# Expert layer of a streaming encoder: v rows of tiles 1 to 5 by a product with the whole v table

## The chip, the core and the metric

The kernel runs on one core of a Trainium2 chip. The metric is the device time of one execution in microseconds.

## The reference

One layer, run for 1024 prompt tokens and 32 sample tokens with the same weights: a retention and a short convolution in parallel heads, an output projection onto the residual, and then the expert layer, which is most of the work:

```python
q = (xb @ wq).reshape(PEER_BLOCK, PEER_HEADS, 2, D_KEY_HALF)
...
top_s, sel = lax.top_k(cand, PEER_TOPK)
eidx = jnp.take_along_axis(cidx, sel, axis=-1)
gate = jax.nn.softmax(top_s.astype(jnp.float32), axis=-1).astype(xb.dtype)
act = jax.nn.gelu(jnp.einsum('td,thkd->thk', xb, u_tab[eidx]))
return jnp.einsum('thk,thkd->td', gate * act, v_tab[eidx])
```

Each token has 8 heads with 16 experts each, 128 in all, out of 16384; an expert is a row of u and a row of v, each 1024 fp32. An index is `i1 * 128 + i2`. A last RMS norm follows.

## The kernel before, in words

Tokens lie on the 128 partitions: tiles 0 to 7 of the prompt, and the sample tile of 32. The expert work is a run of 1056 steps, 128 for each prompt tile and 32 for the sample tile, whose tokens are spread over the partitions four times. In step `g` GpSimd gathers, by an indirect DMA, the u and v rows of one expert for each token of the tile (128 rows of 8 KB, u and v side by side in `uv`) into a row buffer (L985). VectorE multiplies the u half by the normed token and sums it (L2050, one custom instruction and a read of its accumulator). ScalarE takes the gelu of the dot (L1225), multiplies it by the gate (L1241) and scales the v half by it (L1245). TensorE adds that half, transposed in eight pieces, into the PSUM tile `expert_sum` (L1625). When TensorE is through, the buffer is free and GpSimd may gather into it again. There are seven row buffers in `ring`, and from step 616 nine, two of them in `w_out_sb`.

All else is laid between these steps. Each engine has generators that `yield` the step (the code calls it slot) at which they are to go on, and `advance(programs, g)` runs what is due at step `g`; on each engine the order is fixed by these numbers. The projections of the mixing part (L1311, L1344), the output projection (L1406), the queries (L1508) and key scores (L1537) of the later tiles, VectorE's choice of the 16 best (L1852 to L1982) and the weights that SyncE loads for them through three `stream` buffers are such work. Tiles 0 and 1, then 2 to 4, then 5 to 7 with the sample, form groups that are projected together. At the end of a tile `finish(t)` turns the sum back, norms it and SyncE stores it.

```python
for g in range(TOTAL):
    t, k = tile_of(g)
...
    dve.wait_ge(landed[SLOTS[g]], 16 * (lap_of(g) + 1))
    u = row_of(g)[:, 0:D]
    dve.tensor_tensor_reduce(u, u, xn[:, t % 2, :], 1.0, 0.0, ALU.mult, ALU.add,
                             dots[:, SLOTS[g]:SLOTS[g] + 1]).then_inc(dotted, 1)
    advance(programs, g)
```

## Time and profile before

| | us |
|---|---|
| median of 3 executions | 2945.24 (2944.16 to 2946.45) |
| span of the profiled execution | 2941.5 |
| VectorE busy | 2077.7 (71%) |
| TensorE's matmuls busy | 2311.9 (79%) |
| ScalarE busy | 1968.4 (67%) |
| GpSimd busy | 1258.5 (43%) |

The profiled execution is known by its span, from its first to its last instruction; its own time as a run is not listed beside it, so the median is set against the span: 3.7 us lie between them. An engine's busy time is the union of its instructions. Idle time of an engine is put down to what ended it.

### The profile page before, as it was taken

What the parts mean: (1) busy time and instruction counts of PE and PEld (TensorE: products, weight loads), DVE (VectorE), ACT (ScalarE), POOL (GpSimd) and SP (SyncE); (2) the same over time, 40 slices, a digit from 0 to 9 for tenths busy, and PEclk for the clock granted to TensorE, in tenths of its full rate; (3) what the DMA queues carried; (4) which work ended last, traced back from release to release, by engine and by line L of the source; (5) the groups of instructions that cost most, each with busy time, mean ns of one, the idle gap of its engine ahead of it and who ended that gap; (6) DMA issues with size and microseconds to landing.
All of it is one profiled execution on the core that took longest, in us unless ns stands there. A gap on an engine that the chain in (4) does not pass through costs nothing.

```text
span 2941.5 us, 36244 instructions
## 1 busy us (share of the span) xinstructions
PE 2311.9 (79%) x12548; PEld 1815.8 (62%) x12548; DVE 2077.7 (71%) x5143; ACT 1968.4 (67%) x3670; POOL 1258.5 (43%) x1063
## 2 busy tenths in 40 slices
PE   9988988987787777888987888778766666666777
PEld 8877777665565556665665555555655555555556
DVE  3677788675687887777666555788868787766444
ACT  2477666677676777666667676777767666767663
POOL 0233434444343444344444445334444445555653
PEclk9999999999987879999996988988767656666669
DMA  8899999999999999999999999999999999999998
GB/s 340 323 408 404 419 416 407 414 418 421 420 409 415 416 416 411 421 420 409 419 415 410 419 421 420 420 420 420 418 421 421 418 418 413 412 419 410 421 413 338
DMA packets 182055, 1205.73 MB, mean 410 GB/s; under 512 B 21744, under 2 KB 27184, under 8 KB 43504
## 3 DMA queue, kind: packets, MB, share of 16 engines
q0 software_dynamic: 152368, 1107.36, 91.2%
q1 hardware_dynamic: 29264, 95.93, 8.4%
q8 instruction: 99, 1.62, 0.2%
q14 instruction: 84, 0.69, 0.1%
q10 hardware_dynamic: 240, 0.13, 0.0%
HBM read 1198.48 MB, written 4.86 MB: 409 GB/s over the span
## 4 chain that ended last, share of the span: by engine, by line
DMA 42%; PE 22%; DVE 21%; ACT 10%; issue 4%; POOL 1%; SPq 0%; DVEq 0%; ACTq 0%; POOLq 0%
DMA ring<-in_uv,idx 38%; PE expert_sum L1625 9%; DVE ring L2050 9%; ACT ring L1245 4%; DMA w_out_sb<-in_uv,idx 4%; PE x_ps L1406 2%; PE mm L1508 2%; PE mm L1311 1%; ACT weights L1241 1%; PE x_ps L1344 1%; PE mm L1344 1%; DVE pairs_left L1855 1%; ACT L1225 1%; PE x_ps L1311 1%; PE expert_sum L1311 1%
## 5 line engine op out<-in xcount | busy, mean ns | idle before, releaser
L985 POOL DMA_INDIRECT ring<-in_uv,idx x958 | 1137.1, 1187 | 1534.0 <-PE expert_sum L1625 1328.1
L1625 PE MATMUL expert_sum<-ident_sb,ring 128*128 128x128 f32 x7472 | 1222.4, 319 | 516.6 <-ACT ring L1245 513.7
L2050 DVE CUSTOM_DVE_ANT_0 ring<-ring,xn 128x1024 f32<-128x1024 f32 x959 | 1168.1, 1222 | 616.9 <-DMA ring<-in_uv,idx 610.8
L1625 PEld LDWEIGHTS expert_sum<-ident_sb,ring 128*128 128x128 f32 x7472 | 1022.3, 165 | 782.5 <-ACT ring L1245 711.7
L1245 ACT ACTIVATE ring<-ring,weights 128x1024 f32<-128x1024 f32 x934 | 1073.0, 1149 | 30.4
L1225 ACT ACTIVATE dots<-dots 128x1 f32<-128x1 f32 x1056 | 211.4, 200 | 789.8 <-DVE dots L2050 786.9
L1241 ACT ACTIVATE weights<-dots,gate 128x1 f32<-128x1 f32 x1024 | 301.5, 294 | 38.3 <-DVE gate L1994 1.5
L1508 PE MATMUL mm<-xn_in,stream 128*128 128x416 f32 (+1 forms) x500 | 202.9, 531 | 0.0
L1625 PE MATMUL expert_sum<-ident_sb,w_out_sb 128*128 128x128 f32 x720 | 139.2, 358 | 70.0 <-ACT w_out_sb L1245 69.8
L1625 PEld LDWEIGHTS expert_sum<-ident_sb,w_out_sb 128*128 128x128 f32 x720 | 113.6, 186 | 98.7 <-ACT w_out_sb L1245 96.3
L985 POOL DMA_INDIRECT w_out_sb<-in_uv,idx x96 | 115.8, 1206 | 124.9 <-PE expert_sum L1625 110.4
L2050 DVE CUSTOM_DVE_ANT_0 w_out_sb<-w_out_sb,xn 128x1024 f32<-128x1024 f32 x97 | 118.5, 1223 | 68.3 <-DMA w_out_sb<-in_uv,idx 67.7
L1311 PE MATMUL mm<-stream,xn_in 128*128 128x256 f32 (+1 forms) x640 | 166.4, 395 | 0.0
L1311 PEld LDWEIGHTS mm<-stream,xn_in 128*128 128x128 f32 (+1 forms) x640 | 106.8, 182 | 22.4 <-issue 4.2
L1508 PEld LDWEIGHTS mm<-xn_in,stream 128*128 128x128 f32 x500 | 91.4, 204 | 40.9 <-issue 27.1
L1245 ACT ACTIVATE w_out_sb<-w_out_sb,weights 128x1024 f32<-128x1024 f32 x90 | 103.4, 1149 | 2.9
L2050 DVE DVE_READ_ACCUMULATOR2_ANT dots<- 128x1 f32 x1056 | 86.8, 82 | 0.0
L1344 PE MATMUL mm<-xn_in,stream 128*128 128x384 f32 (+1 forms) x232 | 84.3, 496 | 2.6 <-ACT conv_tmp L1028 2.3
L1225 ACT ACT_TABLE_LOAD x50 | 64.2, 1283 | 0.9
L1311 PE MATMUL x_ps<-stream,xn_in 128*128 128x256 f32 x256 | 64.0, 383 | 0.0
L1344 PE MATMUL x_ps<-xn_in,stream 128*128 128x128 f32 (+1 forms) x240 | 60.8, 400 | 0.0
L1571 PE MATMUL mm<-ring,stream 128*128 128x256 f32 x200 | 50.0, 399 | 9.3 <-ACT stream L1231 9.3
(405 smaller groups left out, 2218.3 us busy)
## 6 DMA issues: line engine op xcount, KB each, us to landing
stream<-in_wq SPq DMA_DIRECT2D x21, 1024.0 KB, 11.7
stream<-in_w_conv SPq DMA_DIRECT2D x16, 1024.0 KB, 11.3
stream<-in_w_ret SPq DMA_DIRECT2D x16, 1024.0 KB, 9.5
ring<-in_uv,idx POOLq DMA_INDIRECT x958, 13.9
ring<-in_w_ret SPq DMA_DIRECT2D x6, 1024.0 KB, 12.5
x<-in_x SPq DMA_DIRECT2D x8, 512.0 KB, 8.3
out_y<-xn SPq DMA_DIRECT2D x8, 512.0 KB, 8.2
stream<-in_w_out SPq DMA_DIRECT2D x3, 1024.0 KB, 9.7
```

Source lines behind the costliest of these rows:

```text
L985: pool.indirect_dma_start(row_of(g), None, uv, bass.IndirectOffsetOnAxis(ap=rows, axis=0)).then_inc(landed[SLOTS[g]], 16)
L1225: act.activation(d, d, ACT.Gelu_apprx_tanh).then_inc(gelu_done, 1)
L1241: act.activation(w, d, ACT.Copy, scale=gate[:, t % 5, k:k + 1]).then_inc(weighed, 1)
L1245: act.activation(v, v, ACT.Copy, scale=w).then_inc(scaled, 1)
L1311: ins = pe.matmul(bank[0:n, 0:UNIT], xnj[:, k, at:at + n], weight[k], start=(k == 0), stop=(k == KC - 1))
L1344: ins = pe.matmul(bank[:, 0:columns.stop - columns.start], weight[k], moving, start=(k == 0), stop=(k == KC - 1))
L1406: ins = pe.matmul(x1_ps[0:n, i * 512:(i + 1) * 512], lhsT, w_out_of(j, k)[:, i * 512:(i + 1) * 512], start=(k == 0), stop=(k == KC - 1))
L1508: ins = pe.matmul(query_bank(m, s), weight[s][k], xnT_of_pass(m)[:, k, :], start=(k == 0), stop=(k == KC - 1))
L1571: ins = pe.matmul(last_bank, of[0:rows, 96 - q * DEC:96 - q * DEC + P], values[0:rows, q * QW:(q + 1) * QW], start=begins and q == 0, stop ...
L1625: ins = pe.matmul(expert_sum[:, c * P:(c + 1) * P], row_of(g)[:, D + c * P:D + (c + 1) * P], ident_sb[:, :], is_transpose=True, start=Fals ...
L1855: ins = dve.match_replace(rest, values[:, 0:8], s, LOWEST)
L2050: dve.tensor_tensor_reduce(u, u, xn[:, t % 2, :], 1.0, 0.0, ALU.mult, ALU.add, dots[:, SLOTS[g]:SLOTS[g] + 1]).then_inc(dotted, 1)
```

## The change

For tiles 1 to 5 (`DENSE`, steps 128 to 767) only the u half is gathered: `uv` is seen as 32768 rows of 4 KB, the chosen indices of these tiles are doubled, and eight half buffers in the first four row buffers hold them. VectorE writes the dots of a tile into the columns of `tile_dots`; ScalarE and TensorE do nothing in these steps. In the next tile's time (in tile 6 for tile 5) the spread weights of a tile are built. The indices are split into their two halves, these and the weights (gelu of the dot by the gate) are transposed, and for each token ScalarE makes a one-hot of the first half (`hot_1`, as relu(1 - |iota - i1|)), GpSimd one of the second that carries the weight (`hot_2`), and TensorE multiplies them: the result is that token's 16384 weights, with the second half of the index on the partitions. It goes by groups of four tokens. ScalarE copies it into `staging`, SyncE stores 32 tokens at a time (2 MB, in pieces of 512 B) into a table in DRAM. x1 of tiles 1 to 4 is kept in DRAM too.

From step 826 on TensorE multiplies the spread weights of the five tiles by the whole v table, in 32 chunks of 512 rows: 320 units (chunk, tile, half of the columns) of four matmuls of 128x512, of which `unit_at` puts three into every two steps. VectorE adds each unit from PSUM to the tile's sum, which starts as x1. SyncE loads a chunk of v (2 MB) and the spread weights of each chunk and tile (256 KB). At the end ScalarE and VectorE norm the five sums and SyncE stores them. The three row buffers that the building takes leave six for the full rows of steps 768 to 825, and seven after that. Tiles 0, 6, 7 and the sample are handled as before.

How GpSimd's instructions stand: its queue before, from its first gather on (`in_uv` is the table, `idx` the indices, 128x2048 a full row of each partition).

```order
L985 DMA ring<-in_uv,idx 128x2048 x623
L985 DMA w_out_sb<-in_uv,idx 128x2048 x2
L985 DMA ring<-in_uv,idx 128x2048 x7
L985 DMA w_out_sb<-in_uv,idx 128x2048 x2
L985 DMA ring<-in_uv,idx 128x2048 x7
```

GpSimd's queue in the change, from its first gather into tile 2. The `ring<-ring` rows are the weighted one-hots, which lie in the last three row buffers.

```order
L1180 DMA ring<-in_uv,idx 128x2048 x128
L1159 DMA ring<-in_uv,idx 128x1024 x137
L1130 ISA
L1130 TENSOR_SCALAR ring<-ring 128x128 x4
L1159 DMA ring<-in_uv,idx 128x1024 x3
L1130 TENSOR_SCALAR ring<-ring 128x128 x4
L1159 DMA ring<-in_uv,idx 128x1024 x4
L1130 TENSOR_SCALAR ring<-ring 128x128 x4
L1159 DMA ring<-in_uv,idx 128x1024 x4
```

Full gathers end with tile 0, and from tile 2 on four one-hots stand in the same queue after every three or four gathers, so that a gather waits for them and they for it.

TensorE before, around steps 824 to 832: only the transposes of the rows.

```order
L1625 MATMUL expert_sum<-ident_sb,w_out_sb 128x128 x16
L1625 MATMUL expert_sum<-ident_sb,ring 128x128 x56
L1625 MATMUL expert_sum<-ident_sb,w_out_sb 128x128 x16
```

TensorE in the change, steps 822 to 830 (`tp` is the PSUM pair of the product, `stream` and `ring` hold v, `xn_in` and `qkvg` the spread weights).

```order
L1925 MATMUL expert_sum<-ident_sb,ring 128x128 x32
L1871 MATMUL tp<-stream,xn_in 128x512 x8
L1925 MATMUL expert_sum<-ident_sb,ring 128x128 x8
L1871 MATMUL tp<-stream,xn_in 128x512 x4
L1925 MATMUL expert_sum<-ident_sb,ring 128x128 x8
L1871 MATMUL tp<-stream,xn_in 128x512 x8
L1925 MATMUL expert_sum<-ident_sb,ring 128x128 x8
```

Two units or one now stand ahead of each step's eight transposes.

The diff, cut to its core:

```diff
+DENSE = (1, 2, 3, 4, 5)
+FULL = [t for t in range(TILES + 1) if t not in DENSE]
...
+GROUP4 = 4
+GROUPS4 = P // GROUP4
...
+CHUNK = 4
+CHUNKS = NK // CHUNK
+UNITS = CHUNKS * len(DENSE) * 2
+V_DEEP = 2
+W_DEEP = 6
...
+def build_at(t):
+
+    return (t + 1) * STEPS + 1
+
+
+def group4_at(t, q):
+
+    return build_at(t) + 3 + ((q * 15) // 4 if t != DENSE[-1] else (q * 3) // 2)
+
+
+BUILT = group4_at(DENSE[-1], GROUPS4) + 4
+DENSE_AT = BUILT + 2
+
+
+def unit_at(n):
+
+    return DENSE_AT + (n * 2) // 3
...
+RINGS = [(0, tuple(range(RING))), (DENSE_END, (0, 1, 2, 3, RING, RING + 1)),
+         (BUILT + 2, (0, 1, 2, 3, RING, RING + 1, 4))]
...
+        work = ring[:, 4:7, :].rearrange("p s n -> p (s n)")
+        staging = work[:, 0:NK * BLOCK]
+        hot_1 = work[:, 4096:4608].rearrange("p (t n) -> p t n", t=GROUP4)
+        hot_2 = work[:, 4608:5120].rearrange("p (t n) -> p t n", t=GROUP4)
+        halves_i = work[:, 4608:4864].bitcast(I32).rearrange("p (s n) -> p s n", s=2)
+        halves_f = work[:, 4864:5120].rearrange("p (s n) -> p s n", s=2)
+        tile_dots = work[:, 5120:5376].rearrange("p (b n) -> p b n", b=2)
+        turned_w = work[:, 5376:5760].rearrange("p (s n) -> p s n", s=3)
+        iota_sb2 = work[:, 5760:5888]
+        v_rows = [stream[:, 1:3, :].rearrange("p b (i n) -> p (b i) n", i=2),
+                  ring[:, 5:7, :].rearrange("p b (i n) -> p (b i) n", i=2)]
+        w_rows = [xn_in[:, D + i * CHUNK * P:D + (i + 1) * CHUNK * P] for i in range(4)]
+        w_rows += [qkvg[:, 2, i * CHUNK * P:(i + 1) * CHUNK * P] for i in range(2)]
+        sums = [keys_sb[:, 0:KC, :].rearrange("p b n -> p (b n)"), keys_sb[:, KC:, :].rearrange("p b n -> p (b n)"),
...
+            def store_spread(t):
+
+                for b in range(BLOCKS):
+                    yield group4_at(t, (b + 1) * PER_BLOCK) + 2
+                    i = DENSE.index(t)
+                    sp.wait_ge(w_copied, i * GROUPS4 + (b + 1) * PER_BLOCK)
+                    sp.dma_start(w_spread[i, :, :, b * CHUNK * BLOCK:(b + 1) * CHUNK * BLOCK].rearrange("c p n -> p c n"),
+                                 staging.rearrange("p (c n) -> p c n", c=CHUNKS)).then_inc(w_stored, 16)
...
+            def load_v():
+
+                rows = uv.rearrange("(c i p) n -> c p i n", i=CHUNK, p=P)
+                for c in range(CHUNKS):
+                    yield QUADS_AT_V if c == 0 else BUILT if c == 1 else unit_at((c - 1) * 2 * len(DENSE) - 1) + 1
+                    if c == 0:
+                        sp.wait_ge(queried, 2 * len(PASSES))
+                    elif c == 1:
+                        sp.wait_ge(w_stored, 16 * BLOCKS * len(DENSE))
+                        sp.wait_ge(w_built, GROUPS4 * len(DENSE))
+                    else:
+                        sp.wait_ge(unit_done, (c - 1) * 2 * len(DENSE))
+                    sp.dma_start(v_rows[c % V_DEEP], rows[c][:, :, D:]).then_inc(v_in[c % V_DEEP], 16)
+
+            def load_spread():
+
+                for m in range(CHUNKS * len(DENSE)):
+                    c, i = divmod(m, len(DENSE))
+                    yield BUILT + 1 if m < W_DEEP else unit_at(2 * (m - W_DEEP) + 1) + 1
+                    if m == 0:
+                        sp.wait_ge(w_stored, 16 * BLOCKS * len(DENSE))
+                        sp.wait_ge(queried, 2 * len(PASSES))
+                        sp.wait_ge(chosen, pick(PH - 1, 6) + 1)
+                    elif m >= W_DEEP:
+                        sp.wait_ge(unit_done, 2 * (m - W_DEEP) + 2)
+                    sp.dma_start(w_rows[m % W_DEEP], w_spread[i, c]).then_inc(w_in_rows[m % W_DEEP], 16)
...
+                for q in range(GROUPS4):
+                    yield group4_at(t, q) + 5
+                    if q == 0:
+                        pool.wait_ge(w_turned_copied, 2 * i + 2)
+                        pool.wait_ge(wide_iota, NK // TOPK + 1)
+                    wait(pool, w_built, r + q)
+                    for k in range(GROUP4):
+                        at = GROUP4 * q + k
+                        pool.tensor_scalar(hot_2[:, k, :], iota_sb2[:, :], turned_w[:, 1, at:at + 1],
+                                           turned_w[:, 2, at:at + 1], ALU.is_equal, ALU.mult).then_inc(hot_2_ready, 1)
...
+                if half is not None:
+                    pool.wait_ge(dotted, half + 1)
+                if SLOTS[g] == 4 and g > DENSE_END:
+                    pool.wait_ge(w_stored, 16 * BLOCKS * len(DENSE))
...
+                    pool.indirect_dma_start(half_row_of(g), None, uv.rearrange("n (h d) -> (n h) d", h=2),
+                                            bass.IndirectOffsetOnAxis(ap=idx[:, t % 5, k:k + 1], axis=0)
+                                            ).then_inc(landed[LANDINGS[g]], 16)
...
+                act.activation(tile_dots[:, t % 2, :], tile_dots[:, t % 2, :], ACT.Gelu_apprx_tanh).then_inc(tile_gelu, 1)
...
+                for q in range(GROUPS4 + 1):
+                    yield group4_at(t, q)
+                    if q < GROUPS4:
+                        wait(act, w_built, r + q)
+                        if q == 0:
+                            act.wait_ge(w_turned_copied, 2 * i + 2)
+                        for k in range(GROUP4):
+                            at = GROUP4 * q + k
+                            act.activation(hot_1[:, k, :], iota_sb2[:, :], ACT.Abs,
+                                           bias=turned_w[:, 0, at:at + 1]).then_inc(hot_1_steps, 1)
+                        act.wait_ge(hot_1_steps, (GROUP4 + 1) * (r + q) + GROUP4)
+                        act.activation(hot_1, hot_1, ACT.Relu, bias=one_sb[:, :],
+                                       scale=-1.0).then_inc(hot_1_steps, 1)
+                    if q:
+                        p = q - 1
+                        act.wait_ge(w_built, r + p + 1)
+                        if p % PER_BLOCK == 0:
+                            wait(act, w_stored, 16 * (i * BLOCKS + p // PER_BLOCK))
+                        first = GROUP4 * (p % PER_BLOCK)
+                        act.activation(staging.rearrange("p (c t i) -> p t c i", c=CHUNKS, t=BLOCK)[:, first:first + GROUP4, :, :],
+                                       build_bank(t, p).rearrange("p (t c i) -> p t c i", t=GROUP4, c=CHUNKS),
+                                       ACT.Copy).then_inc(w_copied, 1)
...
+                    pe.wait_ge(hot_1_steps, (GROUP4 + 1) * (r + q + 1))
+                    pe.wait_ge(hot_2_ready, GROUP4 * (r + q + 1))
+                    wait(pe, w_copied, r + q - 1)
+                    for k in range(GROUP4):
+                        ins = pe.matmul(build_bank(t, q)[:, k * NK:(k + 1) * NK], hot_2[:, k, :],
+                                        hot_1[:, k, :], start=True, stop=True)
+                    ins.then_inc(w_built, 1)
...
+                    if i == 0 and h == 0:
+                        pe.wait_ge(v_in[c % V_DEEP], v_in_from[c % V_DEEP] + 16 * (c // V_DEEP + 1))
+                    if h == 0:
+                        pe.wait_ge(w_in_rows[m % W_DEEP], w_in_rows_from[m % W_DEEP] + 16 * (m // W_DEEP + 1))
+                    wait(pe, unit_added, n - 1)
+                    spread_w = w_rows[m % W_DEEP].rearrange("p (t i) -> p t i", i=CHUNK)
+                    for k in range(CHUNK):
+                        ins = pe.matmul(tp[:, n % 2, :], spread_w[:, :, k],
+                                        v_rows[c % V_DEEP][:, k, h * 512:(h + 1) * 512],
+                                        start=(k == 0), stop=(k == CHUNK - 1))
+                    ins.then_inc(unit_done, 1)
...
+                    dve.wait_ge(unit_done, n + 1)
+                    if n == 0:
+                        dve.wait_ge(sums_in, 16 * (len(DENSE) - 1))
+                    if c:
+                        dve.wait_ge(unit_added, n - 2 * len(DENSE) + 1)
+                    half = sums[i][:, h * 512:(h + 1) * 512]
+                    dve.tensor_tensor(half, half, tp[:, n % 2, :], ALU.add).then_inc(unit_added, 1)
...
+                    u = half_row_of(g)
+                    dve.tensor_tensor_reduce(u, u, xn[:, t % 2, :], 1.0, 0.0, ALU.mult, ALU.add,
+                                             tile_dots[:, t % 2, k:k + 1]).then_inc(dotted, 1)
```

## Rows read from the trace of the kernel before

**Rows 1.** The page: DMA share in 40 slices; queues: packets, MB, share.
```profile
DMA  8899999999999999999999999999999999999998
...
q0 software_dynamic: 152368, 1107.36, 91.2%
q1 hardware_dynamic: 29264, 95.93, 8.4%
```

**Rows 2.** The waits: engine, line, what ended it; us, times, longest.
```profile
POOL ring L985 <- PE expert_sum L1625: 1328.1, 807, 5.3
...
DVE ring L2050 <- DMA ring<-in_uv,idx: 610.8, 489, 3.7
...
DVE w_out_sb L2050 <- DMA w_out_sb<-in_uv,idx: 67.7, 55, 2.2
```

**Rows 3.** Windows: bounds, length, busy (count) of PE, PEld, DVE, ACT, POOL; clock; DMA.
```profile
0.00:95.70 95.70, 92.88 (x540) 79.91 (x541) 37.65 (x118) 20.82 (x43) 3.29 (x7) 1.00 0.82 307
...
483.20:830.80 347.60, 286.37 (x1578) 207.62 (x1576) 243.12 (x511) 242.93 (x446) 146.78 (x128) 0.95 1.01 417
830.80:1177.50 346.70, 262.03 (x1426) 205.47 (x1426) 279.12 (x772) 246.41 (x458) 151.03 (x129) 0.83 1.01 413
1177.50:1532.10 354.60, 309.23 (x1755) 230.19 (x1754) 254.90 (x597) 239.09 (x445) 144.41 (x129) 0.97 1.01 417
1532.10:1870.30 338.20, 264.55 (x1367) 188.58 (x1366) 200.42 (x374) 237.32 (x434) 151.78 (x129) 0.85 1.01 418
1870.30:2205.90 335.60, 250.75 (x1324) 191.64 (x1324) 268.21 (x746) 240.67 (x448) 151.20 (x130) 0.82 1.01 420
2205.90:2353.70 147.80, 96.45 (x480) 80.50 (x480) 119.99 (x328) 104.72 (x187) 61.90 (x58) 0.67 1.01 419
2353.70:2894.60 540.90, 375.66 (x1739) 305.76 (x1740) 353.47 (x829) 354.85 (x663) 291.69 (x214) 0.65 1.01 414
```

**Rows 4.** Groups, each shape apart: gathers and dots (busy us, mean ns | idle before).
```profile
L985 POOL DMA_INDIRECT ring<-in_uv,idx x958 | 1137.1, 1187 | 1534.0 <-PE expert_sum L1625 1328.1 <-PE expert_sum L1311 91.0 <-issue 57.8
...
L2050 DVE CUSTOM_DVE_ANT_0 ring<-ring,xn 128x1024 f32<-128x1024 f32 x959 | 1168.1, 1222 | 616.9 <-DMA ring<-in_uv,idx 610.8
L2050 DVE DVE_READ_ACCUMULATOR2_ANT dots<- 128x1 f32 x1056 | 86.8, 82 | 0.0
```

**Rows 5.** Timeline of 3.7 us on GpSimd and VectorE: start, length, instruction.
```profile
1000.72 0.94 POOL L985 DMA_INDIRECT ring<-in_uv,idx  x1 [1.46 <-PE expert_sum L1625]
1002.88 1.48 POOL L985 DMA_INDIRECT ring<-in_uv,idx  x1 [1.23 <-PE expert_sum L1625]
...
1002.32 1.23 DVE L2050 CUSTOM_DVE_ANT_0 ring<-ring,xn 128x1024 f32<-128x1024 f32 x1
```

**Rows 6.** Groups, each shape apart: the nearest rows for the new instructions.
```profile
L971 POOL DMA_INDIRECT ring<-in_uv,spare x1 | 0.9, 936 | 1.5 <-PE mm L1571 1.5
L2123 POOL MEMSET const-float32-0.0<- 128x1 f32 x1 | 0.1, 99 | 0.2 <-issue 0.2
...
L1724 DVE SCALAR_TENSOR_TENSOR conv_tmp<-conv_tmp,par 128x128 f32<-128x128 f32 x16 | 5.6, 352 | 0.6
...
L1781 DVE TENSOR_TENSOR qkvg<-mm,decay_p_sb 128x512 f32<-128x512 f32 x8 | 5.5, 688 | 2.1 <-PE mm L1367 2.1
...
L1153 ACT ACTIVATE scores<-tp 128x256 f32<-128x256 f32 x36 | 13.3, 368 | 1.9 <-PE tp L1537 1.9
...
L1056 ACT ACTIVATE turn<-tp 128x512 f32<-128x512 f32 x16 | 8.6, 589 | 0.4 <-PE tp L1359 0.4
```

**Rows 7.** DMA issues: KB and median us from issue to landing.
```profile
w_out_sb<-in_w_out SPq DMA_DIRECT2D x1, 2048.0 KB, 23.7
```

**Rows 8.** TensorE: matmuls of 512 columns, weight loads, and a step's eight transposes.
```profile
63.83 3.60 PE L1420 MATMUL x_ps<-w_out_sb,qkvg 128*128 128x512 f32 x8
...
L1420 PEld LDWEIGHTS x_ps<-w_out_sb,qkvg x16: 190/190/192, 63.7 to 72.0; 128*128 128x128 f32 x16
...
1001.57 1.04 PE L1625 MATMUL expert_sum<-ident_sb,ring 128*128 128x128 f32 x8
```

More of the change, by code:

```diff
@@ L60, with is_dense, full_before, landing_of @@
 QUADS_IN = 0
+QUADS_AT_V = 780
 SPLIT = 2
-RINGS = [(0, RING), (88 * RING, RING + 2)]
+DENSE = (1, 2, 3, 4, 5)
+FULL = [t for t in range(TILES + 1) if t not in DENSE]
+HALVES = 8
+DENSE_FIRST = DENSE[0] * STEPS
+DENSE_END = (DENSE[-1] + 1) * STEPS
+ROW_SLOTS = RING + 2
+GROUP4 = 4
+GROUPS4 = P // GROUP4
+BLOCK = 32
+BLOCKS = P // BLOCK
+PER_BLOCK = BLOCK // GROUP4
+CHUNK = 4
[11 more added lines that the diff above has]
+    return DENSE_AT + (n * 2) // 3
+def is_dense(g):
+    return DENSE_FIRST <= g < DENSE_END
+RINGS = [(0, tuple(range(RING))), (DENSE_END, (0, 1, 2, 3, RING, RING + 1)),
+         (BUILT + 2, (0, 1, 2, 3, RING, RING + 1, 4))]
 def slot_of(g):
     first, slots = [r for r in RINGS if r[0] <= g][-1]
-    return (g - first) % slots
+    return (g - first) % HALVES if is_dense(g) else slots[(g - first) % len(slots)]
 SLOTS = [slot_of(g) for g in range(TOTAL)]
-def lap_of(g):
-    return SLOTS[:g].count(SLOTS[g])
-def same_slot_before(g):
-    return max((b for b in range(max(0, g - 2 * RING), g) if SLOTS[b] == SLOTS[g]), default=None)
+def full_before(g):
+    return sum(not is_dense(b) for b in range(min(g, TOTAL)))
+def landing_of(g):
+    return SLOTS[g] // 2 + SLOTS[g] % 2 * (HALVES // 2) if is_dense(g) else SLOTS[g]
+LANDINGS = [landing_of(g) for g in range(TOTAL)]
+def lap_of(g):
+    return LANDINGS[:g].count(LANDINGS[g])
+def halves_of(g):
+    return (SLOTS[g],) if is_dense(g) else (2 * SLOTS[g], 2 * SLOTS[g] + 1)
+def steps_before(g):
+    near = {}
+    for b in range(max(0, g - 3 * STEPS * len(DENSE)), g):
+        for half in halves_of(b):
+            near[half] = b
+    found = {near[half] for half in halves_of(g) if half in near}
+    return (max((b for b in found if not is_dense(b)), default=None),
+            max((b for b in found if is_dense(b)), default=None))
+def full_index(t):
+    return sum(u < t for u in FULL)
 def rows_of(t):
@@ L165, in sums_before_out @@
 def sums_before_out(t):
-    return sum(end_of(u) < out_at(t) for u in range(TILES + 1))
+    return sum(end_of(u) < out_at(t) for u in FULL)
 TURNS = [(x_turn_at(t), t, "x") for t in range(TILES + 1)]
@@ L916, in store_y, with store_sums @@
+            def store_sums():
+                yield unit_at(UNITS) + 4
+                for i, t in enumerate(DENSE):
+                    sp.wait_ge(end_step, len(DENSE) + 3 + i)
+                    sp.dma_start(y[t * P:(t + 1) * P, :], sums[i]).then_inc(end_out, 16)
             def store_y(t):
@@ new lines, in end_sums @@
+            def end_sums():
+                yield unit_at(UNITS) + 2
+                act.wait_ge(unit_added, UNITS)
+                for i in range(len(DENSE)):
+                    act.activation(v_rows[i // CHUNK][:, i % CHUNK, :], sums[i], ACT.Square,
+                                   accum_out=end_stat[:, 0, i:i + 1]).then_inc(end_step, 1)
+                act.wait_ge(end_step, len(DENSE))
+                act.activation(end_stat[:, 0, :], end_stat[:, 0, :], ACT.Sqrt, bias=eps_sb[:, :],
+                               scale=1.0 / D).then_inc(end_step, 1)
@@ new lines, in dense @@
+            def dense():
+                for n in range(UNITS):
+                    m, h = divmod(n, 2)
+                    c, i = divmod(m, len(DENSE))
+                    yield unit_at(n)
+                    if n == 0:
+                        pe.wait_ge(keyed_copied, len(SCORES) - 1)
+                        pe.wait_ge(xnT_copied, 2 * len(TURNS))
+                    if i == 0 and h == 0:
[9 more added lines that the diff above has]
+                    ins.then_inc(unit_done, 1)
@@ L1582, in _ @@
+            programs = started(warm_up(), rstd_row(), *[back(t) for t in FULL], *[build(t) for t in DENSE], dense(),
                                *[projection(j) for j in range(len(GROUPS))],
@@ new lines, in end_sums @@
+            def end_sums():
+                yield unit_at(UNITS) + 3
+                dve.wait_ge(end_step, len(DENSE) + 1)
+                dve.reciprocal(end_stat[:, 1, :], end_stat[:, 0, :]).then_inc(end_step, 1)
+                dve.wait_ge(end_step, len(DENSE) + 2)
+                for i in range(len(DENSE)):
+                    dve.scalar_tensor_tensor(sums[i], sums[i], end_stat[:, 1, i:i + 1], g_fin_sb[:, :],
+                                             ALU.mult, ALU.mult).then_inc(end_step, 1)
```

224 lines of the change are left out of this document (174 added, 50 removed).

## The prediction

> **What bounds the kernel now.** I read the page's slices first: the DMA engines are busy for nine tenths or more of every slice but the first two and the last [rows 1]; no compute engine has such a row. The queue lines say whose traffic it is: the gathers' queue holds 91.2% of the engines' time for 1107 MB, so one of 1056 gathers costs 0.912 x 2941.5 / 1056 = 2.54 us; everything else is 96 MB in 8.4%, which is 388 GB/s [rows 1]. The list of waits closes the circle: GpSimd waits 1328 us for TensorE to free a row buffer, and at the other end of the chain VectorE waits 611 + 68 us for rows to land [rows 2]; ScalarE and TensorE follow VectorE. The first cause is the landing. So time before is bytes; the question is what bounds each stretch when the bytes are fewer. I cut the span at the steps where the change has its seams [rows 3]: tile 1, tiles 2 to 5 (one window each), steps 768 to 825 and steps 826 to 1038. In all of them the DMA share is full before; only the first 96 us and what follows step 1038 differ.
>
> **Bytes after.** 640 gathers of half size save 640 x 1.27 = 813 us of DMA time. The v table (67.1 MB), the spread weights written (41.9 MB) and read (41.9 MB) and the kept x1 (4 MB) are 155 MB, at 388 GB/s 400 us. If all stayed DMA bound the span would fall by 413 us. It can't, since the saving lies in tiles 1 to 5 and nearly all of the addition behind step 768, where nothing is saved. Each part therefore has to be costed with its own limit.
>
> **Tiles 1 to 5, VectorE's side.** It still makes each dot: 1.22 us and 0.08 us for the read-out [rows 4]. Nothing else goes from it but the final scaling of each of the five sums, which moves to the end. Its busy time in the five windows is 243.1, 279.1, 254.9, 200.4 and 268.2, in sum 1245.7 of 1722.7 us [rows 3]; that is the floor. Waits for other engines come on top: in the span VectorE is idle for 863.8 us, 678.5 of them for rows; of the other 185 us, 58 lie before the first dot (95.70 - 37.65), and 127 on 2040 busy us are 6%, which I keep.
>
> **Tiles 2 to 5, GpSimd's side.** Here are the weighted one-hots of tiles 1 to 4, 512 instructions of 128x128 (those of tile 5 stand in tile 6). Where GpSimd stands in the way is seen in the timeline [rows 5]: the gather issued at 1000.72, beside a reduce that reads one operand, takes 0.94 us; the one issued at 1002.88, inside a dot that ends at 1003.55, takes 1.48, which is the 0.67 us left of the dot and 0.81. A gather's issue waits until the dot that is running ends. The smaller gathers cost GpSimd no less: those of 4 KB rows take 0.94 us too [rows 6], so the halved rows save nothing there. A one-hot reads SBUF as well, so I let it wait as the gather does. Its own length isn't in the trace: below it lies a memset of one column on GpSimd, 0.1 us, above it a gather's issue, 0.94 us; the nearest row is VectorE's 128x128 operation, 0.35 us [rows 6], and I take that. Whether it then holds up a dot, no row shows: dots keep 1.22 us beside gathers. Bounds are 0 and 0.35 us for each, and I take the upper, since a reader that must wait for a dot is likely to make a dot wait too. The Trainium skill (SBUF — State Buffer, the sections on ports) says that VectorE with two SBUF inputs and a reading GpSimd instruction exclude each other for the whole instruction, whichever came first; by that rule the upper end holds, by the row alone the sum would be 190 us less.
>
> VectorE then needs (1002.6 + 512 x 0.35) x 1.06 = 1253 us for tiles 2 to 5. GpSimd per step: a gather of 0.94 to 1.30 and 0.35 + 0 to 1.22 for the one-hot: 1.29 at best and 2.87 at worst, where each of its instructions stands behind a full dot, against VectorE's 2.45. In the middle it is hidden. Tile 1 has no one-hots: 243.1 x 1.06 = 258. ScalarE and TensorE lose their per-step work here and don't bind; DMA needs 1.27 us a step and 22 us a tile for weights written (8.4 MB). Together **1511 us for 1722.7: -212**.
>
> **Steps 768 to 825.** Full rows again, and tile 5's one-hots in 48 steps, a group of four each step and a half. ScalarE: 104.7 us for 58 steps before [rows 3], 1.8 a step; a group adds four instructions of 128 columns and two of 512. By its 128x256 at 0.37 and 128x512 at 0.59 [rows 6] these are 4 x 0.26 + 2 x 0.59 = 2.2, or 1.5 a step: 3.3 us. GpSimd: 1.2 and 2.67 x (0.35 + 0.3) = 2.9. DMA: 2.54 and 8.4 MB of stores over 48 steps, 0.45: 3.0. Three loads of equal size, coupled through one set of one-hots and a staging buffer that must be stored before it is filled again, with six row buffers in place of nine: I take 4.0 us a step, 232 us, between 3.3 (191) and 4.7 (273). Behind it TensorE stands at the first unit of the product until the last 2 MB store has landed and the first weights have been read back; a 2 MB load takes 23.7 us from issue to landing [rows 7], and I take 25 us in all, between 10 and 40. **257 for 147.8: +109.**
>
> **Steps 826 to 1038: the product with the whole table.** 320 units of four matmuls of 128x512, three units every two steps. Eight such matmuls take 3.60 us, 0.45 each, and a step's eight transposes 1.04 [rows 8]. TensorE: 6 x 0.45 + 1.04 = 3.7 us a step, at the full clock: before, the granted clock was 0.65 here, with TensorE busy for 70% of the time, but 1.00 in the first 96 us, where it was busy for 97% [rows 3]; I expect the latter. DMA: 2.54 + 1.5 x (67.1 + 41.9) MB / 320 / 388 GB/s = 2.54 + 1.32 = 3.86, the larger. VectorE: 1.66 us a step before (353.5 / 213), and 1.5 additions of 0.69 [rows 6], hence 2.7; ScalarE 1.7. With two engines within 4% of each other and seven buffers, 5% are lost to their coupling: 4.05 x 213 = **863 for 540.9: +322**. The bounds are 3.86 (822) and 4.4 (937). The rest, with five squares and five scalings on engines with slack, and five stores of 0.5 MB: 46.9, **+2**.
>
> **Sum.** -212 + 109 + 322 + 2 = +221 on 2941.5, so a span of 3162.5; the median lies 3.7 us above the profiled span, so **3166 us**, 7.5% slower. In short: the change takes 336 MB out of a stretch that at once finds another limit, and 109 MB of streams and 1280 x 0.45 = 576 us of matmul into one that has none to spare.
>
> **Rivals.**
> - *Faster: nothing excludes anything.* One-hots run beside dots without touching them. Then tiles 1 to 5 take 1245.7 x 1.06 = 1320 (-402), steps 768 to 825 take 3.3 x 58 + 15 (+59), the product is at its DMA floor, 822 (+281), +2: -60, 2885 us. For it: the 959 dots have a mean of 1.22, that of the one beside the gather in [rows 5], and GpSimd's issue is 1.19 in the mean [rows 4], 0.25 over the free one. Against it: [rows 5], and that it needs all three at once. It decides for faster once tiles 1 to 5 need less than 2.1 us a step with 3.9 us in the product; VectorE's floor is 1245.7 / 640 = 1.95 (mine: 2.36 and 4.05).
> - *Slower: GpSimd becomes the bound.* VectorE has rows waiting whenever four one-hots come in a row, so each stands behind a full dot: 2.87 x 512 + 258 = 1727 for tiles 1 to 5 (+4), and the rest as above: +437, 3382 us. It decides once a gather and a one-hot together take over 2.45 us. For it: the issues' mean is 1.19 already, with VectorE at dots for 45% of the time (157 of 350 us a tile: 128 x 1.22); at 2.45 us a step it is at them for half. Against: at that pace VectorE is idle for a seventh of the time.
> - *Slower: TensorE becomes the bound of the product.* Its stationary operand steps by four elements; the loads shown step by one and take 0.19 us [rows 8]. If a column that steps by four costs as much as four that step by one, a load is 0.76, when a step takes 6 x 0.76 + 1.04 = 5.6 us, 1193 us in all (+652), 3496 us. The nearest row is the 0.19 itself, which its matmul's 0.45 us hides more than twice over. The Trainium skill (SBUF — State Buffer, the note on cachelines) has 16-byte lines and a penalty for each access that crosses into a new one; by it every fp32 element here is on its own line. No run shows it, and the chance stands at one in twelve. A clock left at 0.65 would come out alike: 3.7 / 0.65 = 5.7 us a step.
>
> **Chances.** My own course 0.62, VectorE untouched 0.13, GpSimd bound 0.15, TensorE bound 0.08, about even 0.02. A range of 2930 to 3400 us leaves out the last and the better part of the fast case. A measurement of this kernel tells 0.2% from no change: faster 0.13, same 0.02, slower 0.85.
>
> **What would show it.** In tiles 2 to 5 dots of 1.22 us with waits for GpSimd's one-hots between them, a pitch near 2.45 us, DMA share about 0.7; gathers' issues of up to 2 us; one-hots in the order of 0.35 us alone. In steps 826 to 1038 a DMA share near 0.95, TensorE's clock at 1.00, loads of stationary operands under 0.45 us, a pitch near 4.05. A pitch below 2.2 in the first, or far from 4 in the second, proves the sum wrong.

## The result

The changed kernel takes 3875.26 us (median of 4, 3867.77 to 3877.41) against 2945.01 us (4 executions, 2944.16 to 2946.45): 1.315 times as long, 95% interval 1.3132 to 1.3169. The forecast was 3166 us with a range of 2930 to 3400. The sign was right, the size was not: of the 930 us that were lost 221 were foreseen, a quarter.

### The profile page after: what moved, and what is told of

Read it like the earlier page. It is cut to its first block, busy times and chain, and to the rows that moved or that the text cites. A ratio compares the mean times of both kernels' runs of the same rounds, so it can differ in the third digit from the quotient of the medians.

```text
span 3873.0 us, 34448 instructions
## 1 busy us (share of the span) xinstructions
PE 2868.9 (74%) x11203; PEld 2132.2 (55%) x11203; DVE 2306.7 (60%) x5493; ACT 1282.2 (33%) x2681; POOL 2054.4 (53%) x1703
## 4 chain that ended last, share of the span: by engine, by line
PE 45%; POOL 11%; issue 10%; DMA 6%; ACT 4%; DVE 4%; SPq 0%; ACTq 0%; DVEq 0%; POOLq 0%
PE tp L1871 29%; POOL ring L1130 6%; POOL ring L1159 5%; PE expert_sum L1925 5%; DMA w_spread<-ring 4%; PE expert_sum L1851 3%; PE mm L1559 2%; PE mm L1756 2%; DMA ring<-in_uv,idx 2%; PE x_ps L1654 2%; ACT ring L1423 2%; DVE ring L2407 1%; PE mm L1818 1%; ACT ring L1426 1%; PE x_ps L1851 1%
## 5 line engine op out<-in xcount | busy, mean ns | idle before, releaser
L1130 POOL TENSOR_SCALAR ring<-ring 128x128 f32<-128x128 f32 x640 | 794.2, 1248 | 39.6 <-PE x_ps L1851 19.6
L1851 PE MATMUL expert_sum<-ring 128*128 128x128 f32 x1024 | 225.4, 390 | 627.2 <-issue 558.5
L1851 PEld LDWEIGHTS expert_sum<-ring 128*128 128x128 f32 x1024 | 195.6, 285 | 682.3 <-issue 651.7
L1925 PE MATMUL expert_sum<-ident_sb,ring 128*128 128x128 f32 x2480 | 350.5, 289 | 86.0 <-ACT ring L1493 85.1
L1871 PE MATMUL tp<-stream,xn_in 128*128 128x512 f32 x864 | 392.3, 604 | 28.9 <-DMA xn_in<-w_spread 28.9
L1925 PEld LDWEIGHTS expert_sum<-ident_sb,ring 128*128 128x128 f32 x2480 | 308.8, 150 | 165.3 <-ACT ring L1493 100.3
L1871 PE MATMUL tp<-ring,xn_in 128*128 128x512 f32 x864 | 390.1, 601 | 0.0
L1493 ACT ACTIVATE ring<-ring,weights 128x1024 f32<-128x1024 f32 x310 | 356.2, 1149 | 10.1
L1423 ACT ACTIVATE ring<-ring 128x128 f32<-128x128 f32 x640 | 203.4, 390 | 394.3 <-PE expert_sum L1851 341.1
L1871 PEld LDWEIGHTS tp<-stream,xn_in 128*128 128x128 f32 x864 | 261.7, 310 | 120.4 <-issue 32.7
L1871 PEld LDWEIGHTS tp<-ring,xn_in 128*128 128x128 f32 x864 | 261.2, 310 | 87.2
```

Source lines behind the costliest of these rows:

```text
L1130: pool.tensor_scalar(hot_2[:, k, :], iota_sb2[:, :], turned_w[:, 1, at:at + 1], turned_w[:, 2, at:at + 1], ALU.is_equal, ALU.mult).then_in ...
L1423: act.activation(hot_1[:, k, :], iota_sb2[:, :], ACT.Abs, bias=turned_w[:, 0, at:at + 1]).then_inc(hot_1_steps, 1)
L1493: act.activation(v, v, ACT.Copy, scale=w).then_inc(scaled, 1)
L1851: ins = pe.matmul(build_bank(t, q)[:, k * NK:(k + 1) * NK], hot_2[:, k, :], hot_1[:, k, :], start=True, stop=True)
L1871: ins = pe.matmul(tp[:, n % 2, :], spread_w[:, :, k], v_rows[c % V_DEEP][:, k, h * 512:(h + 1) * 512], start=(k == 0), stop=(k == CHUNK - 1))
L1925: ins = pe.matmul(expert_sum[:, c * P:(c + 1) * P], row_of(g)[:, D + c * P:D + (c + 1) * P], ident_sb[:, :], is_transpose=True, start=Fals ...
```

## The profile after

The page of the changed kernel: TensorE's matmuls, GpSimd, the granted clock and the DMA share in 40 slices, and the queues.

```profile
PE   9889878344366674655553255599999999999998
...
POOL 0343256598889988998989777311221112222212
PEclk9999988666678886767766566699999999999999
DMA  8999988767577676767666767767667667667666
...
q0 software_dynamic: 152368, 771.82, 54.8%
q1 hardware_dynamic: 152592, 251.13, 18.0%
```

Where [rows 1] had a full DMA row, no slice behind the fifth is full now. GpSimd holds the stretch from the ninth to the 22nd slice, TensorE everything behind the 26th. Both engines were the bound of a rival of the forecast, though TensorE for another reason than the one given there. The windows, cut at the same steps as [rows 3] (tiles 1, 2, 3, 4, 5, steps 768 to 825, steps 826 to 1038, the rest; columns as there):

```profile
488.40:756.90 268.50, 176.58 (x547) 101.22 (x545) 238.69 (x509) 32.39 (x56) 162.88 (x133) 0.82 0.85 307
756.90:1119.30 362.40, 169.54 (x635) 126.33 (x635) 285.65 (x784) 103.44 (x253) 314.62 (x255) 0.68 0.65 220
1119.30:1478.10 358.80, 246.45 (x960) 169.61 (x961) 258.81 (x601) 103.86 (x245) 320.16 (x256) 0.84 0.71 245
1478.10:1829.20 351.10, 184.76 (x616) 111.99 (x615) 202.62 (x378) 102.11 (x241) 315.17 (x257) 0.70 0.71 237
1829.20:2197.20 368.00, 149.30 (x524) 104.77 (x523) 273.79 (x749) 95.56 (x237) 320.49 (x256) 0.65 0.64 217
2197.20:2464.50 267.30, 142.37 (x717) 128.54 (x718) 122.87 (x329) 174.62 (x375) 185.18 (x185) 0.67 0.73 266
2464.50:3814.80 1350.30, 1321.43 (x4276) 973.74 (x4275) 558.70 (x1147) 356.64 (x662) 274.74 (x215) 0.99 0.68 251
3814.80:3873.00 58.20, 44.16 (x167) 34.84 (x165) 28.40 (x45) 22.48 (x68) 17.38 (x15) 0.91 0.70 270
```

| stretch | before | forecast | after | pitch after |
|---|---|---|---|---|
| tile 0 and what is ahead of it | 483.2 | 483.2 | 488.4 | |
| tile 1 | 347.6 | 258 | 268.5 | 2.10 |
| tiles 2 to 5 | 1375.1 | 1253 | 1440.3 | 2.81 |
| steps 768 to 825 | 147.8 | 257 | 267.3 | 4.61 |
| steps 826 to 1038 | 540.9 | 863 | 1350.3 | 6.34 |
| the rest | 46.9 | 49 | 58.2 | |

Of the 709 us between forecast and result, 487 lie in the product's stretch and 187 in tiles 2 to 5; the four other lines make up 35. "Steps 768 to 825" is not as good a hit as it looks: the forecast of 257 was 232 for the steps (4.0 us each) and 25 for TensorE's wait ahead of the first unit. That wait falls behind step 826, in the product's 1350.3 us, so the 267.3 us are the steps alone.

What GpSimd does, its groups in the changed kernel over the whole span (busy us, mean ns of one, idle before); the 640 gathers of half rows take in tile 1, the 640 one-hots steps 768 to 825:

```profile
L1159 POOL DMA_INDIRECT ring<-in_uv,idx x640 | 762.3, 1191 | 270.4 <-issue 158.3 <-DVE ring L2407 92.6 <-PE expert_sum L1925 18.9
L1130 POOL TENSOR_SCALAR ring<-ring 128x128 f32<-128x128 f32 x640 | 794.2, 1248 | 39.6 <-PE x_ps L1851 19.6 <-PE expert_sum L1851 8.2 <-ACT ring L1410 6.5
```

and the same line by its durations (min/median/max in ns):

```profile
L1130 POOL TENSOR_SCALAR ring<-ring x640: 780/805/4635, 763.9 to 2447.6; 128x128 f32<-128x128 f32 x160
```

A one-hot takes 0.80 us when nothing is in its way, and 1.25 in the mean over all 640. Over tiles 2 to 5 alone the mean is 1.31, with 1.18 for the gather. With 0.33 us of idle time for each step (1440.3 - 1270.4 busy in four tiles, over 512 steps) that is the pitch of 2.8.

What lengthens a one-hot can be counted in the trace. The 237 beside which no dot ran took 0.80 us in the mean. The 226 that began while a dot was running took 1.82, and the middle one of them ended 0.67 us behind the end of that dot. The same holds for the issue of a gather in the kernel before: 449 began while a dot was running, and half of them ended 0.811 to 0.813 us behind its end. So one row of [rows 5] had the rule right for the gather. The timeline shows both kinds, four one-hots in 4.34 us and two in 3.30:

```profile
1303.75 1.09 POOL L1159 DMA_INDIRECT ring<-in_uv,idx  x1 [0.31 <-issue]
1304.88 4.34 POOL L1130 TENSOR_SCALAR ring<-ring 128x128 f32<-128x128 f32 x4
1309.38 1.03 POOL L1159 DMA_INDIRECT ring<-in_uv,idx  x1 [0.17 <-issue]
...
1316.07 3.30 POOL L1130 TENSOR_SCALAR ring<-ring 128x128 f32<-128x128 f32 x2
```

The waits of tile 3, the longest first (1119.3 to 1478.1 us; engine, what it was about to work on <- what came last, us in total, times, longest), say the same from the other side:

```profile
PEld expert_sum L1851 <- issue: 93.7, 24, 8.3
...
DVE ring L2407 <- DMA ring<-in_uv,idx: 64.2, 32, 5.8
```

L1851 is the matmul with a one-hot. The 24 waits ahead of it, up to 8.3 us, are put down to "issue", with no releaser shown; the code has it wait there for `hot_1_steps`, `hot_2_ready` and `w_copied`, and which of them came last is for the experiments. VectorE's wait for rows here is not a wait for bytes: with the DMA share at 0.64 to 0.71 the rows are late because they were asked for late.

TensorE in the product's stretch, first the timeline (start, us, engine, line, entries):

```profile
2495.01 10.03 PE L1871 MATMUL tp<-stream,xn_in 128*128 128x512 f32 x16 [28.87 <-DMA xn_in<-w_spread]
...
3002.51 1.04 PE L1925 MATMUL expert_sum<-ident_sb,w_out_sb 128*128 128x128 f32 x8
3003.39 7.15 PE L1871 MATMUL tp<-stream,xn_in 128*128 128x512 f32 x16
3010.37 1.04 PE L1925 MATMUL expert_sum<-ident_sb,w_out_sb 128*128 128x128 f32 x8
```

and the loads of the unit's line by their durations (min/median/max in ns):

```profile
L1871 PEld LDWEIGHTS tp<-stream,xn_in x864: 307/308/332, 2495.0 to 3766.6; 128*128 128x128 f32 x173
```

Two units are eight matmuls in the code and 16 entries here, in 7.15 us: 0.45 us an entry as in [rows 8], and 0.89 a matmul. Behind the first wait the stretch is TensorE's without a gap: 1321 us busy and 28.9 of wait are the 1350, at a clock of 0.99.

## The experiments

All are edits of the changed kernel, which stands at 3875 us. A pitch is the mean time from one dot to the next in a stretch; those of the runs are read as in the table above.

### Half of the product's matmuls

```diff
-                    for k in range(CHUNK):
+                    for k in (0, CHUNK - 1):
```

> Leaves out two of the four matmuls of each unit of the product with the v table (the sums of tiles 1 to 5 lack half of the experts); every load, gather and addition stays. Theory (TensorE bounds the product, since one fp32 matmul of 512 columns is two entries of 0.45 us in the trace and costs 0.89 us): the pitch of steps 826 to 1038 falls from 6.34 us to what the DMA engines need, 0.68 x 6.34 = 4.3 us, or a little over, and the span from 3873 by some 400 us to 3450 to 3500. Rival (the units wait for their loads or for VectorE's additions, TensorE only shows busy): under 100 us. Tiles 1 to 5 do not move.

Measured: 3366 us. Steps 826 to 1038 take 844.1 us, a pitch of 3.96, tiles 2 to 5 are where they were. Windows of this run (tiles 2 to 5 together, steps 768 to 825, steps 826 to 1038):

```profile
760.70:2188.20 1427.50, 753.21 (x2732) 513.32 (x2732) 1022.71 (x2508) 405.25 (x975) 1260.73 (x1021) 0.72 0.69 232
2188.20:2466.50 278.30, 150.36 (x715) 136.84 (x715) 123.14 (x331) 174.33 (x375) 183.76 (x185) 0.62 0.74 260
2466.50:3310.60 844.10, 790.27 (x3004) 584.23 (x3005) 551.85 (x1147) 356.63 (x663) 273.90 (x216) 0.97 1.00 400
```

The stretch lost 506 us, its additions by VectorE, loads and gathers all being there. TensorE bounded it. The DMA share is now 1.00. What I had wrong in the expectation is the floor: 0.68 of 6.34 is 4.3 us, but the DMA engines need 3.9; a share taken at a slack pace overstates the need.

### A quarter of them

```diff
-                    for k in range(CHUNK):
+                    for k in range(1):
...
-                                        start=(k == 0), stop=(k == CHUNK - 1))
+                                        start=True, stop=True)
```

> Leaves out three of the four matmuls of each unit (the sums lack three quarters of the experts), all else stays. TensorE would need 1.5 x 0.89 + 1.04 = 2.4 us a step. Theory: the DMA engines are the next bound at about 4.3 us a step, so this run is no more than 30 us faster than the one with half the matmuls, 3430 to 3480, and shows the floor of the stretch. Rival (TensorE bounds at every size): another 280 us.

Measured: 3344 us, 22 us under the run with half. The same windows:

```profile
2462.30:3289.40 827.10, 569.91 (x2368) 396.98 (x2369) 549.55 (x1146) 356.03 (x662) 274.39 (x216) 0.86 1.01 408
```

The DMA floor of the stretch is 827.1 / 213 = 3.88 us a step. The forecast's 3.86 had been worked out from [rows 1], so bytes and rate together held; only TensorE's side of the comparison was wrong.

### Stationary operands read with a step of one

```diff
-                        ins = pe.matmul(tp[:, n % 2, :], spread_w[:, :, k],
+                        ins = pe.matmul(tp[:, n % 2, :], w_rows[m % W_DEEP][:, k * P:(k + 1) * P],
```

> The stationary operand of the product is read as 128 neighbouring columns instead of every fourth (the products are of the wrong weights, so the outputs of tiles 1 to 5 are others). Theory: the weight load falls from 0.308 us to 0.19 us and nothing else moves, since it lies beside a pass of 0.43 us: 3873 within 15 us. Rival (strided weight loads bound TensorE): the pitch of steps 826 to 1038 falls by 6 to 12 times 0.12 us, 150 to 300 us in all.

Measured: 3840 us, 35 us less, 25 of them in the product's stretch (1325.4 us).

```profile
L1871 PEld LDWEIGHTS tp<-stream,xn_in x864: 190/190/338, 2485.3 to 3732.1; 128*128 128x128 f32 x173
```

The step of four costs 0.12 us a load, not the fourfold. Nearly all of it is hidden beside the matmul entries, which follow each other every 0.43 us: 25 us over 1280 matmuls are 0.02 each. It fell a little outside both expectations, but the rival that put the bound in the loads is out.

### One one-hot of four on GpSimd

```diff
-                    for k in range(GROUP4):
+                    for k in range(1):
                         at = GROUP4 * q + k
                         pool.tensor_scalar(hot_2[:, k, :], iota_sb2[:, :], turned_w[:, 1, at:at + 1],
...
-                        ins = pe.matmul(build_bank(t, q)[:, k * NK:(k + 1) * NK], hot_2[:, k, :],
+                        ins = pe.matmul(build_bank(t, q)[:, k * NK:(k + 1) * NK], hot_2[:, 0, :],
```

> GpSimd makes one weighted one-hot per group of four, which all four matmuls of the group use (spread weights of three tokens in four are wrong); 160 instructions instead of 640. Theory (GpSimd bounds tiles 2 to 5: a gather 1.19 and a one-hot 1.25 with its waits, 2.6 to 2.8 us): the pitch there falls from 2.81 to VectorE's 2.1 to 2.3, -250 to -350 us, and steps 768 to 825 get 40 us shorter: 3480 to 3590. Rival (the chain GpSimd, TensorE, ScalarE per group bounds by its handshakes): less than 100 us.

Measured: 3559 us. Tiles 2 to 5:

```profile
759.00:1917.60 1158.60, 699.44 (x2732) 482.25 (x2732) 995.88 (x2507) 403.80 (x975) 844.83 (x636) 0.75 0.84 286
```

282 us less (1440.3 to 1158.6), a pitch of 2.26, with VectorE at 86%. The handshakes of the 160 groups all remain, so it is GpSimd's work on the one-hots that bounded. With a quarter of them the stretch is VectorE's, and 995.9 us of its work took 1.16 times as long. Steps 768 to 825 take 232.3 us in this run, 4.0 us a step.

### Narrow one-hots

```diff
-                        pool.tensor_scalar(hot_2[:, k, :], iota_sb2[:, :], turned_w[:, 1, at:at + 1],
+                        pool.tensor_scalar(hot_2[:, k, 0:32], iota_sb2[:, 0:32], turned_w[:, 1, at:at + 1],
```

> GpSimd's one-hots write 32 columns of the 128 (most of the spread weights are stale, the sums of tiles 1 to 5 are wrong); the number of instructions stays. Theory (its 0.80 us alone is length by column): an instruction falls to about 0.3 us alone, tiles 2 to 5 gain up to 512 x 0.5 = 250 us and end at 3620 to 3700. Rival (0.80 us is a fixed cost of the instruction): 3873 within 40 us.

Measured: 3698 us, inside the theory's range, with tiles 2 to 5 at 2.50 us a step.

```profile
L1130 POOL TENSOR_SCALAR ring<-ring x640: 460/477/5201, 765.1 to 2271.5; 128x32 f32<-128x32 f32 x160
```

Medians of 0.477 us for 32 columns and 0.805 for 128: about 0.37 us fixed and 3.4 ns a column.

### One by one

```diff
                     for k in range(GROUP4):
                         at = GROUP4 * q + k
+                        yield group4_at(t, q) + 2 + (k if t != DENSE[-1] else k // 3)
```

with the `yield group4_at(t, q) + 5` ahead of it changed to `+ 2`.

> GpSimd's four one-hots of a group no longer stand in a row: in tiles 2 to 5 one stands before each gather (in steps 768 to 825 up to four again), three steps sooner in its queue. Nothing is left out. Theory (the length counts: 0.80 us alone for a one-hot and 0.94 for a gather, and what each waits for dots): the pitch of 2.81 moves by less than 0.15 us, 3873 within 80 us. Rival (the rows of four cause the waits, since each one-hot of a row stands behind a full dot): the mean one-hot falls from 1.25 to 1.0 us or less and the pitch to 2.5, -150 us.

Measured: 3984 us, slower by 108, outside both. The mean one-hot did fall, to 1.10 us, but the gathers rose and GpSimd, now with less lead, waits for TensorE to be through with the group before:

```profile
L1160 POOL DMA_INDIRECT ring<-in_uv,idx x640 | 822.9, 1286 | 212.7 <-issue 115.9 <-DVE ring L2408 77.6 <-PE expert_sum L1926 18.9
L1131 POOL TENSOR_SCALAR ring<-ring 128x128 f32<-128x128 f32 x640 | 704.4, 1101 | 272.2 <-PE expert_sum L1852 139.3 <-PE x_ps L1852 77.0 <-ACT ring L1411 36.5
```

Over the kernel the one-hots gave back 90 us and the gathers took 61. What grew beside that was GpSimd's idle time, most of it waits for TensorE. Two things were changed at once, so it isn't a clean test of the rows of four, and whether another placement would help stays open.

### One-hots on VectorE

```diff
-            programs = started(*[build(t) for t in DENSE])
+            programs = started()
...
+                for q in range(GROUPS4):
+                    yield group4_at(t, q)
...
+                    wait(dve, w_built, r + q)
+                    for k in range(GROUP4):
+                        at = GROUP4 * q + k
+                        dve.tensor_scalar(hot_2[:, k, :], iota_sb2[:, :], turned_w[:, 1, at:at + 1],
+                                          turned_w[:, 2, at:at + 1], ALU.is_equal, ALU.mult).then_inc(hot_2_ready, 1)
```

> The weighted one-hots are made by VectorE at the step of their group, GpSimd only gathers. Nothing is left out. A 128x128 tensor_scalar on VectorE costs about 0.29 us by the shortest of its kind before. Theory: tiles 2 to 5 are bound by VectorE at (2.0 + 0.31) x 1.06 = 2.45 us a step, -185 us, and steps 768 to 825 gain 40: about 3650. Rival (what bounds there is the handshake of each group): about 3870, and the pitch stays at 2.8.

Measured: 3663 us (3654 and 3672), 212 less than the changed kernel; against the kernel before 1.2435, interval 1.2353 to 1.2517. Tiles 2 to 5 and the new line:

```profile
754.80:2000.60 1245.80, 720.26 (x2732) 493.72 (x2732) 1114.21 (x3020) 404.50 (x975) 642.89 (x509) 0.74 0.79 266
...
L2369 DVE TENSOR_SCALAR ring<-ring x640: 327/342/551, 768.6 to 2227.0; 128x128 f32<-128x128 f32 x160
```

2.43 us a step, close to the forecast's 2.45 for a stretch bound by VectorE with 0.35 us a one-hot. The same instruction has a median of 0.34 us on VectorE and of 0.80 on GpSimd.

### One-hots on ScalarE

```diff
-            programs = started(*[build(t) for t in DENSE])
+            programs = started()
...
+                        for k in range(GROUP4):
+                            at = GROUP4 * q + k
+                            act.activation(hot_2[:, k, :], iota_sb2[:, :], ACT.Abs, scale=-1.0,
+                                           bias=turned_w[:, 1, at:at + 1]).then_inc(hot_2_ready, 1)
...
+                        act.activation(hot_2, hot_2, ACT.Relu, bias=one_sb[:, :],
+                                       scale=-1.0).then_inc(hot_2_ready, 1)
...
+                            act.activation(hot_2[:, k, :], hot_2[:, k, :], ACT.Copy,
+                                           scale=turned_w[:, 2, at:at + 1]).then_inc(hot_2_ready, 1)
```

> The weighted one-hots are made by ScalarE (four of Abs, one Relu, four scalings per group), GpSimd only gathers. Nothing is left out. Theory: ScalarE, busy for 103 of 360 us a tile, takes 32 x 3.7 = 118 us more a tile beside the others; VectorE bounds tiles 2 to 5 at 2.15 to 2.3 us a step, -260 to -340 us; in steps 768 to 825 ScalarE needs some 5.8 us a step and costs 60 us more: 3590 to 3670. Rival (VectorE was the bound all along): no gain over the run with the one-hots on VectorE.

Measured: 3752 us, a miss. Tiles 2 to 5 and steps 768 to 825:

```profile
762.80:2027.70 1264.90, 719.92 (x2717) 493.07 (x2717) 985.14 (x2507) 804.92 (x2125) 644.52 (x508) 0.74 0.78 262
2027.70:2345.60 317.90, 159.80 (x731) 145.35 (x731) 120.88 (x330) 276.86 (x666) 57.06 (x57) 0.63 0.64 226
```

The second stretch came as expected (+51 us, ScalarE at 87%). In the first no engine is above 78%, and the pitch is 2.47 in place of 2.2. What bounds it was not settled. The trace shows that it isn't the rows: of VectorE's 280 idle us in this stretch only 20 ended with a row of the table, while 112 ended with a result of ScalarE and 104 with one of TensorE. A likely candidate, not tested, is that whatever else is due on ScalarE waits behind nine instructions of a group in a row, and VectorE for that. A second one, not tested either, is the single staging buffer: ScalarE stood for 146.9 us, up to 30.9 at a time, until a store had emptied it, with all its later work behind.

### Shared between VectorE and GpSimd, and shared with half the product

```diff
-                    for k in range(GROUP4):
+                    for k in range(2, GROUP4):
                         at = GROUP4 * q + k
                         pool.tensor_scalar(hot_2[:, k, :], iota_sb2[:, :], turned_w[:, 1, at:at + 1],
...
+                    for k in range(2):
+                        at = GROUP4 * q + k
+                        dve.tensor_scalar(hot_2[:, k, :], iota_sb2[:, :], turned_w[:, 1, at:at + 1],
+                                          turned_w[:, 2, at:at + 1], ALU.is_equal, ALU.mult).then_inc(hot_2_by_dve, 1)
```

> Of each four weighted one-hots VectorE makes two and GpSimd two. Nothing is left out. GpSimd then needs 1.19 + 0.3 + 0.53 x 1.25 = 2.15 us a step with its gaps, VectorE (2.0 + 0.53 x 0.3) x 1.06 = 2.3. Theory (the stretch is bound by the busier of the two): tiles 2 to 5 at 2.3 us a step against 2.43 with all on VectorE and 2.81 with all on GpSimd, so 3590 us, the fastest of the complete kernels after the change. Rival (each group's handshakes bound): 2.5 or more, 3680 us.

Measured: 3668 us (3661 and 3674), the same as with all of them on VectorE; 2.43 us a step, VectorE at 86%, GpSimd at 79%. The theory that the busier engine sets the pace gave 2.3. Neither engine is full, and a group's matmuls need both shares: TensorE waited 264.8 us in this run for VectorE's part of the one-hots and 108.9 us in tiles 2 to 5 for GpSimd's. That this handshake is what keeps the pitch at 2.43 is argued, not tested.

> The shared one-hots and two of the four matmuls of each unit left out (the sums of tiles 1 to 5 lack half of the experts): what is left when both bounds are taken off. Theory: 3590 - 505 = 3085, within 30 us, still slower than the kernel before at 2945, since the product's stretch then has the DMA engines at 3.9 us a step where there were 2.54, and tiles 1 to 5 gain less than that costs. Rival: under 2945, and the idea would only need a cheaper matmul.

Measured: 3169 us, 84 above the theory, nearly all of which the shared run had already missed; with one-hots on ScalarE and half the product, below, 3243. Steps 826 to 1038 take 842.5 us in it.

> One-hots on ScalarE, and two of four matmuls of each unit left out (the sums lack half of the experts): both bounds taken away at once. Theory: the two gains add, 3873 - 270 - 400 = 3200, within 60 us; still above the kernel before, since the stretch with the product is then at the DMA engines' 4.3 us a step against 2.54 before.

The two gains add: 3668 - 506 = 3162 against 3169, and 3752 - 506 = 3246 against 3243. So the two bounds lie one behind the other in time and share nothing. With half the product and the one-hots shared the kernel is still 7.6% behind the one before. The nearest to both bounds gone is an estimate: the run with one one-hot of four with its product's stretch replaced by that of the run with a quarter of the matmuls, 3559 - 1349 + 827 = 3037 us, still 3% behind. No version that was complete came below a median of 3663 us, and a matmul at half the price would not have brought it below 2945.

## Why the prediction was wrong

**The term of the product was mis-sized, and it carried the size of the result.** The step "Eight such matmuls take 3.60 us, 0.45 each" counts entries of the trace as matmuls. The eight entries of L1420 in [rows 8] are its matmuls with `w_out_sb`, and the loop `for k in range(KC)` in `first_out` has four of those (`KEPT` is 4) in its first part. A full fp32 matmul leaves two entries, each of 0.43 to 0.45 us for 512 columns; only the transposes (`is_transpose`) leave one: 7472 entries for the 934 steps on `ring` before, eight each. So a step needed 6 x 0.89 + 1.04 = 6.4 us in place of 3.7, and 6.34 were measured, 6.2 of them TensorE at work. TensorE and the DMA engines were never within 4% of each other. The runs with half and a quarter of the matmuls show it: 844 and 827 us in place of 1350.

**The rest of that sum held, but for one hit by luck.** The DMA floor of 3.86 us a step came out at 3.88, the wait ahead of the first unit (first row of TensorE's timeline above) at 28.9 us for 25, the clock at 0.99 for 1.00. Steps 768 to 825 came to 267 us for 257, but at 4.61 us a step where 4.0 was forecast, near the upper bound of 4.7; the two figures lie close only because the forecast counted the wait there. The one-hots are part of the excess, since with one of four the steps came down to 4.0; the rest of what bounds them stays open. The rival "TensorE becomes the bound" had a pitch of 5.6 to 5.7 us, nearer to the 6.34, and its cause wrong: a load with a step of four takes 0.31 us, not 0.76. The Trainium skill's note on cachelines (SBUF — State Buffer) has the direction right, and the measured price is 0.12 us a load, 25 us in the stretch.

**Tiles 2 to 5 went to the rival that was given 0.15.** "I take the nearest row, VectorE's 0.35 us": GpSimd needs 0.80 for its 128x128 operation, near the upper bound of 0.94 that stood in the text. With a mean wait of 0.50 the one-hot costs 1.31 in these tiles, and GpSimd, not VectorE, sets the pitch: 2.81, against the 2.87 of the rival and 2.45 of the forecast. "In the middle it is hidden" was the sentence that failed; the middle of 1.29 and 2.87 was no measurement. That the rival's number fits so well is luck. Its one-hot was 0.35 long and waited 1.22 us, with no idle time; the real one is 0.80 long and waits 0.50, with 0.33 idle. Nor was 2.87 the worst case that it was called: by the reading of [rows 5] a gather behind a full dot takes 1.22 + 0.81 = 2.03 us, not the 1.30 in the sum.

**The hold on the dots was counted and isn't there.** I charged VectorE 0.35 us for each one-hot, 190 us in all. Dots of half rows took 1.246 us in the mean, those of full rows 1.221:

```profile
L2407 DVE CUSTOM_DVE_ANT_0 ring<-ring,xn 128x1024 f32<-128x1024 f32 x640 | 786.5, 1246 | 278.0 <-DMA ring<-in_uv,idx 271.9
...
L2413 DVE CUSTOM_DVE_ANT_0 ring<-ring,xn 128x1024 f32<-128x1024 f32 x332 | 404.3, 1221 | 164.8 <-DMA ring<-in_uv,idx 162.5
```

The first group takes in tile 1, which has no one-hots, with a mean of 1.220; in tiles 2 to 5 the mean is 1.25. So a dot grew by 0.03 us, 16 us in all. GpSimd waits for VectorE; hardly the other way. By the Trainium skill's rule (SBUF — State Buffer, "Who interferes with whom") whichever starts first should have blocked the other for a whole instruction, and the measurement decides: here it bound one side.

The sum for VectorE was off the other way in its waits. Tile 1 came close, 268.5 us for 258, but the run with one one-hot of four has tiles 2 to 5 bound by VectorE at 1.16 times its busy time, where the forecast had 1.06. A hold that isn't there and waits that were too small stood against each other in the 1253 us.

**What held in the argument:** the saving lay where another engine took over at once, and the addition where nothing was spare; even without both bounds the idea stays behind, by the estimate above.

## What to carry to other kernels

Before a matmul's time is taken from a trace, count the entries of one loop whose matmuls the code gives: fp32 leaves two for each, a transpose one. Work that moves to another engine is priced on that engine, and where the trace has no such instruction there, the range stays as wide as its bounds. And bytes that are saved while one engine holds the pace and added where the DMA engines do are no saving, whatever their balance over the kernel says.
